# The order of GpSimd's gathers and the units of VectorE's additions in a decoder layer with an expert feed-forward

## The chip, the core and the metric

The kernel runs on one core of one Trainium2 chip. The metric is the device time of one execution in microseconds; a kernel's number is the median of its runs. Lines are those of the kernel before.

## What is computed

One decoder layer on 256 tokens of width 2048, float32 in and out. The first half (an input projection, two kinds of causal convolution, an output projection, a layer norm) gives x1. The second half is a feed-forward block with 16,384 experts, of which every token picks 16 in each of 8 heads:

```python
experts = e1 * N_KEYS + e2            # 128 picks for each token
act = gelu(einsum('td,thkd->thk', x_tok, peer_u[experts]))
coef = act * softmax(top_s)
f = einsum('thk,thkd->td', coef, peer_v[experts])
x = layer_norm(ALPHA * x1 + f, ln2_g, ln2_b)
```

## The kernel before

**Units.** All weights come in units of 128 x 1024 floats (512 KB), loaded by SyncE into a ring of four (`raw`). A product keeps float32 precision by splitting each unit: ScalarE rounds it (`w_hi`, L575), VectorE (L815) or GpSimd (L500) makes the rest (`w_lo`), and TensorE multiplies both parts. Everything is written against a unit number u. VectorE splits unit u + 3 at its turn u, so it is at most three units ahead of TensorE; both rings have four places.

**The up stage** (U_UP on) multiplies x1 with all 16,384 columns of `u_w`, tile by tile of 128 experts. For the first 192 tokens the activations are kept dense and multiplied with dense gates. For the last 64 tokens (SPARSE) ScalarE puts the activations of every expert into `stage` and from there into DRAM (`act_spill`).

**The down stage** (U_DOWN to U_END, 256 units) multiplies the dense coefficients of 192 tokens with `v_w`: 32 groups of four tiles, 8 units a group, each unit ten matmuls of 128x512 (L1576 to L1581). Coefficients of the next group are split at each group's first unit (ScalarE L728 and L729, VectorE L1234 and L1235). The last four groups are ordered by columns instead (U_LAST = U_DOWN + 224), so that results are folded and normalized early.

**The last 64 tokens** take another way in that stage. Each has 128 picks, laid out as 64 picks (PICKS) over two halves of the partitions. For pick k GpSimd issues indirect DMAs:

- `gather_acts` (L536, DMA at L538): one DMA fetches the 128 activations of pick k (4 bytes for each partition) from `act_spill`. Sixteen of them (PICKS_IN) raise one semaphore, `act_in[n]`. VectorE waits for it once per sixteen picks (`pick_coefs`, L1278) and makes sixteen columns of coefficients at once (L1279).
- `gather_rows` (L525, DMAs at L532): four DMAs fetch the row of `v_w` for each partition, 512 floats each, into one of four buffers (`rows`, ROWS = 4). Row k waits until pick k - 4 is done with the buffer. The first two rows are fetched in the up stage.

VectorE adds the row, times its coefficient, to `picked` in `pick(k)` (L1281; L1288 for k = 0, else L1291). The pick stands in VectorE's instruction stream at unit `pick_unit(k)`, behind the split of unit u + 3 and the coefficient split, if one is there:

```python
            for u in range(U_DOWN, U_END):
                if u + LEAD < U_END:
                    lo(u + LEAD, u + LEAD)
                ...
                if u in coef_at:
                    coef_lo(coef_at[u])
                for k in range(PICKS):
                    if pick_unit(k) == u:
                        pick(k)
```

GpSimd does nothing else in this stage until the final layer norm. Its order is written out by hand: rows 0 and 1, acts 0 to 15, rows 2 and 3; then acts 16 to 31 and rows 4 to 11; acts 32 to 47 and rows 12 to 19; acts 48 to 63 and rows 20 to 63. When all 64 picks are done (ScalarE waits for it in `split_high(0)`, L761, in unit U_LAST + 11), `picked` is split and folded into the result by matmuls.

Of the kernel before, what the change touches and what calls it, by code (L numbers as in the profile page):

```python
# [33 lines left out]
PICKS = HEADS * TOPK // HALVES  # L34
ROWS = 4
PICKS_IN = 16
# [24 lines left out]
U_DOWN = U_UP + 2 * N_KEYS  # L61
# [15 lines left out]
U_LAST = U_DOWN + 2 * NCH * G_LAST  # L77
# [28 lines left out]

def pick_unit(k):

    return U_DOWN + 14 + (U_LAST - U_DOWN - 16) * k // PICKS

PC_B = 0
PC_CW = PC_B + 2 * CONF_TILES + 3 * SC_TILES
# [8 lines left out]
def build(nc, x_t, x_nat, w_in, w_out, w_q, u_w, v_w, params, sub_keys, b_out, ln1_g, ln1_b, ln2_g, ln2_b, out):  # L121
# [11 lines left out]
    with ctx:  # L133
        def sb(name, shape, dt, where=ctx):
            return where.enter_context(nc.sbuf_tensor(name, shape, dt))

        def sem(name):
            return ctx.enter_context(nc.semaphore(name))
# [119 lines left out]
        sp_idx = sb("sp_idx", [P, 1 + NCH, PICKS], u32)  # L258
# [117 lines left out]
        act_in = [sem(f"act_in{i}") for i in range(PICKS // PICKS_IN)]  # L376
# [25 lines left out]
        def vector_takes(u):  # L402


            if u < U_CONV:
                return True
            if U_Q <= u < U_ROUTED:
                return False
            return u >= U_ROUTED or u % 2 == 0
# [67 lines left out]
        @block.gpsimd  # L477
        def _(pool):
            nc.gpsimd.iota(iota[:, :], [[1, P]], base=0, channel_multiplier=0,
                           allow_small_or_imprecise_dtypes=True).then_inc(iota_done, 1)  # L480
            pool.wait_ge(iota_done, 1)
            nc.gpsimd.tensor_copy(iota_t[:, :, :], iota[:, :].unsqueeze(2).to_broadcast([P, P, INNER]))\
                .then_inc(iota_done, 1)
            nc.gpsimd.memset(ident[:, :], 0.0).then_inc(pool_done, 1)
            nc.gpsimd.memset(ones[:, :], 1.0 / (CONF_TILES * P)).then_inc(pool_done, 1)
            nc.gpsimd.memset(apad[:, :, 0:TAPS - 1], 0.0).then_inc(pool_done, 1)
            nc.gpsimd.memset(scpad[:, 0:SC_TAPS - 1], 0.0).then_inc(pool_done, 1)
            pool.wait_ge(pool_done, 4)
            nc.gpsimd.affine_select(out=ident[:, :], in_=ident[:, :], compare_op=ALU.not_equal, fill=1.0,
                                    base=0, pattern=[[-1, P]], channel_multiplier=1).then_inc(pool_done, 1)  # L490

            def stream_rest(first, end):

                assert first % RAW == 0 and end % RAW == 0
                with pool.Fori(first // RAW, end // RAW) as i:
                    for s in range(RAW):
                        if not vector_takes(end - RAW + s):

                            pool.wait_ge(hi_done, RAW * i + s + 1)
                            nc.gpsimd.tensor_tensor(w_lo[s][:, :], raw[:, s, :], w_hi[s][:, :].bitcast(f32),  # L500
                                                    ALU.subtract).then_inc(lo_done[s], SPLIT)

            first_loop = -(-U_CONV // RAW) * RAW
            for u in range(U_CONV, first_loop):
                if not vector_takes(u):
                    pool.wait_ge(hi_done, u + 1)
                    nc.gpsimd.tensor_tensor(w_lo[u % SPLIT][:, :], raw[:, u % RAW, :],
                                            w_hi[u % SPLIT][:, :].bitcast(f32),
                                            ALU.subtract).then_inc(lo_done[u % SPLIT], SPLIT)
            stream_rest(first_loop, U_Q)  # L510
            stream_rest(U_Q, U_UP)


            pool.wait_ge(x1_out, 16)
            nc.gpsimd.iota(sp_tok[:, 0:1], [[1, 1]], base=0, channel_multiplier=1,
                           allow_small_or_imprecise_dtypes=True).then_inc(tok_done, 1)
            nc.gpsimd.memset(fold_f, 0.0).then_inc(fold_made, 1)
            pool.wait_ge(fold_made, 1)
            nc.gpsimd.tensor_tensor(fold_f[:, SPARSE:2 * SPARSE], ident[:, 0:SPARSE], ident[:, SPARSE:P],
                                    ALU.add).then_inc(fold_made, 1)  # L520
            pool.wait_ge(fold_made, 2)
            nc.gpsimd.tensor_copy(fold[:, :], fold_f).then_inc(fold_made, 1)
            stream_rest(U_UP, U_ROUTED)

            def gather_rows(k):  # L525

                if k >= ROWS:
                    pool.wait_ge(picked_done, k - ROWS + 1)
                elif k >= 2:
                    pool.wait_ge(used, USED0 + U_DOWN)  # L530
                for j in range(NCH):
                    nc.gpsimd.indirect_dma_start(  # L532
                        rows[k % ROWS][:, j * DCH:(j + 1) * DCH], None, v_rows,
                        bass.IndirectOffsetOnAxis(sp_idx[:, 1 + j, k:k + 1], 0)).then_inc(rows_in[k % ROWS], 16)

            def gather_acts(n):  # L536
                for k in range(PICKS_IN * n, PICKS_IN * (n + 1)):
                    nc.gpsimd.indirect_dma_start(  # L538
                        sp_act[:, k:k + 1], None, act_dram,
                        bass.IndirectOffsetOnAxis(sp_idx[:, 0, k:k + 1], 0)).then_inc(act_in[n], 16)  # L540

            pool.wait_ge(idx_done, 1)
            pool.wait_ge(sel_tr, 1)
            for k in range(2):
                gather_rows(k)
            pool.wait_ge(stage_out, 16 * (N_KEYS // STORED))
            gather_acts(0)
            for k in range(2, ROWS):
                gather_rows(k)
            for n in range(1, PICKS // PICKS_IN):  # L550
                gather_acts(n)
                for k in range(ROWS + 8 * (n - 1), ROWS + 8 * n):
                    gather_rows(k)
            for k in range(ROWS + 8 * (PICKS // PICKS_IN - 1), PICKS):
                gather_rows(k)

            pool.wait_ge(ln2_in, 32)
            for n, (b, d) in enumerate(LN2_POOL):
                sl = slice(d * DCH, (d + 1) * DCH)
                pool.wait_ge(normed, 2 * n + 2)  # L560
                nc.gpsimd.tensor_tensor(res[:, b, sl], res[:, b, sl], ln2g[:, sl], ALU.mult).then_inc(pool_ln, 1)
                pool.wait_ge(pool_ln, n + 1)
                nc.gpsimd.tensor_tensor(res[:, b, sl], res[:, b, sl], ln2b[:, sl], ALU.add).then_inc(fin_pool, 1)
# [240 lines left out]
        def _(dve):  # L804
# [529 lines left out]
# [3 lines that stand above are left out]
                if u == U_DOWN:  # L1337
                    gate_tile_of(N_KEYS - 1)
# [5 lines that stand above are left out]
                if u in split_at and u < U_END - 2 * LAST:  # L1344
                    split_low(split_at[u])
                j, n = (u - U_LAST) // (2 * LAST), (u - U_LAST) % (2 * LAST)
                if u >= U_LAST and 1 <= j < NCH - 1 and n < 2:
                    dve.wait_ge(used, USED0 + U_LAST + 2 * LAST * j)
                    if n == 0:
                        dve.wait_ge(res_in, 16)  # L1350
                        added = add_down(0, j - 1)
                    else:
                        chunk_stats(0, j - 1, chain[0], x2_in)
                if u >= U_LAST and j == 2 and n == 5:
                    add_folded(0)
# [340 lines left out]
```

## Time and profile before

| | us |
|---|---|
| median of 3 runs | 1906.56 |
| lowest and highest run | 1905.19, 1913.26 |
| profiled execution | 1898.23 |
| its span, first to last instruction | 1896.4 |
| TensorE busy | 1779.9 (94%) |
| VectorE busy | 1363.7 (72%) |
| GpSimd busy | 670.2 (35%) |

The mean granted clock of TensorE is 0.978 of its full 2.4 GHz. A busy time is the time in which an engine had an instruction running. Matmuls overlap and their ends are modelled, so the sum over lines is more than the busy time. "Issue" is time in which an engine waited for nothing that the profile shows. The down stage lies between about 1175 us and the end.

### The profile page before, as it was taken

To read this page: it belongs to the slowest core of one execution; us is meant where nothing else is said; L and a number is where in the kernel's file an instruction comes from. 1 tells how busy PE (TensorE), PEld (TensorE's weight loads), DVE (VectorE), ACT (ScalarE), POOL (GpSimd) and SP (SyncE) were. 2 spreads that over 40 slices of the span, in tenths; PEclk is the share of its full clock that TensorE was granted. 3 is DMA by queue.
4 is the path that set the end of the run, shared out by engine and by line. 5 is a ranking of instruction groups with operands and counts; after the bars stand their busy time and mean duration, and the time that the engine had idled before them with its cause. 6 is when DMAs were issued, how large, how long until landed. Compare 5 with 4: busy or idle time off the path is not lost.

```text
span 1896.4 us, 33625 instructions
## 1 busy us (share of the span) xinstructions
PE 1779.9 (94%) x12090; PEld 1627.9 (86%) x12090; DVE 1363.7 (72%) x1903; ACT 855.4 (45%) x1212; POOL 670.2 (35%) x425
## 2 busy tenths in 40 slices
PE   8999999899999999999999999969695999999996
PEld 8999978899999999999999999847574777777875
DVE  7998985699937777777764445557483787888866
ACT  5544444444444444444444444524242445444443
POOL 0000024678961000000000000677786787777201
PEclk9999999999999999999999999989897999999999
DMA  7665556555566555555556565769695999999863
GB/s 277 225 211 191 184 167 215 189 173 175 170 209 229 183 182 186 183 181 188 181 189 194 191 193 191 230 201 332 220 346 187 383 350 369 332 348 366 293 210 114
DMA packets 137934, 433.27 MB, mean 228 GB/s; under 512 B 34304, under 2 KB 34432, under 8 KB 136320
## 3 DMA queue, kind: packets, MB, share of 16 engines
q1 hardware_dynamic: 97440, 359.97, 55.9%
q0 software_dynamic: 22528, 67.16, 9.7%
q10 hardware_dynamic: 17888, 5.26, 1.2%
q8 instruction: 30, 0.49, 0.1%
q14 instruction: 48, 0.39, 0.1%
HBM read 423.83 MB, written 8.39 MB: 228 GB/s over the span
## 4 chain that ended last, share of the span: by engine, by line
PE 71%; POOL 11%; issue 8%; DMA 5%; DVE 4%; ACT 2%; SPq 0%; DVEq 0%; POOLq 0%; ACTq 0%
PE psum L1409 18%; PE psum L1410 18%; PE psum L1411 18%; POOL rows L532 5%; DMA raw<-in_v_w_dram 4%; POOL sp_act L538 4%; PE psum L1576 3%; PE psum L1578 2%; PE psum L1577 2%; PE psum L1580 2%; PE psum L1581 2%; DVE w_lo L815 2%; PE psum L1543 1%; PE psum L1453 1%; PE psum L1455 1%
## 5 line engine op out<-in xcount | busy, mean ns | idle before, releaser
L575 ACT ACTIVATE w_hi<-raw 128x1024 fp32r<-128x1024 f32 x652 | 691.2, 1061 | 936.4 <-PE psum L1411 484.3
L815 DVE TENSOR_TENSOR w_lo<-raw,w_hi 128x1024 fp32r<-128x1024 f32 x568 | 688.6, 1224 | 310.3 <-ACT w_hi L575 303.3
L1409 PE MATMUL psum<-xt_hi,w_hi 128*128 128x256 f32 x2944 | 827.1, 281 | 15.5 <-DVE xt_lo L829 9.3
L1410 PE MATMUL psum<-xt_lo,w_hi 128*128 128x256 f32 x2944 | 824.6, 280 | 0.0
L1411 PE MATMUL psum<-xt_hi,w_lo 128*128 128x256 f32 x2944 | 823.7, 280 | 0.0
L1409 PEld LDWEIGHTS psum<-xt_hi,w_hi 128*128 128x128 f32 x2944 | 555.2, 189 | 17.4 <-issue 11.5
L1411 PEld LDWEIGHTS psum<-xt_hi,w_lo 128*128 128x128 f32 x2944 | 555.1, 189 | 0.0
L1410 PEld LDWEIGHTS psum<-xt_lo,w_hi 128*128 128x128 f32 x2944 | 555.0, 189 | 0.0
L532 POOL DMA_INDIRECT rows<-in_v_w_dram,sp_idx x256 | 364.4, 1423 | 148.1 <-issue 101.6
L538 POOL DMA_INDIRECT sp_act<-act_spill,sp_idx x64 | 78.6, 1228 | 626.2 <-DMA act_spill<-stage 585.5
L1576 PE MATMUL psum<-w_hi,c_hi 128*128 128x512 f32 x504 | 204.3, 405 | 78.9 <-DVE w_lo L815 76.7
L500 POOL TENSOR_TENSOR w_lo<-raw,w_hi 128x1024 fp32r<-128x1024 f32 x82 | 211.4, 2593 | 74.1 <-ACT w_hi L575 73.6
L1291 DVE SCALAR_TENSOR_TENSOR picked<-rows,sp_coef,picked 128x2048 f32<-128x2048 f32 x63 | 148.4, 2356 | 76.0 <-DMA rows<-in_v_w_dram,sp_idx 51.0
L1577 PE MATMUL psum<-w_lo,c_hi 128*128 128x512 f32 x504 | 201.8, 400 | 0.0
L1578 PE MATMUL psum<-w_hi,c_lo 128*128 128x512 f32 x504 | 201.5, 400 | 0.0
L1580 PE MATMUL psum<-w_hi,c_both 128*128 128x512 f32 x504 | 201.2, 399 | 0.0
L1581 PE MATMUL psum<-w_lo,c_both 128*128 128x512 f32 x504 | 201.0, 399 | 0.0
L1576 PEld LDWEIGHTS psum<-w_hi,c_hi 128*128 128x128 f32 x504 | 96.1, 191 | 109.9 <-DVE w_lo L815 84.0
L1578 PEld LDWEIGHTS psum<-w_hi,c_lo 128*128 128x128 f32 x504 | 96.3, 191 | 23.4
L1580 PEld LDWEIGHTS psum<-w_hi,c_both 128*128 128x128 f32 x504 | 96.1, 191 | 23.5 <-DVE w_lo L815 0.2
L1581 PEld LDWEIGHTS psum<-w_lo,c_both 128*128 128x128 f32 x504 | 95.8, 190 | 23.2
L1577 PEld LDWEIGHTS psum<-w_lo,c_hi 128*128 128x128 f32 x504 | 96.3, 191 | 22.2
(193 smaller groups left out, 1165.1 us busy)
## 6 DMA issues: line engine op xcount, KB each, us to landing
raw<-in_u_w_dram SPq DMA_DIRECT2D x256, 512.0 KB
raw<-in_v_w_dram SPq DMA_DIRECT2D x256, 512.0 KB
raw<-in_w_in_dram SPq DMA_DIRECT2D x80, 512.0 KB
raw<-in_w_out_dram SPq DMA_DIRECT2D x32, 512.0 KB
raw<-in_w_q_dram SPq DMA_DIRECT2D x32, 512.0 KB
act_spill<-stage ACTq DMA_DIRECT2D x32, 128.0 KB, 2.3
rows<-in_v_w_dram,sp_idx POOLq DMA_INDIRECT x256
xt_raw<-in_x_t_dram SPq DMA_DIRECT2D x4, 512.0 KB, 7.5
```

The source lines that it names most:

```text
L500: nc.gpsimd.tensor_tensor(w_lo[s][:, :], raw[:, s, :], w_hi[s][:, :].bitcast(f32), ALU.subtract).then_inc(lo_done[s], SPLIT)
L532: nc.gpsimd.indirect_dma_start(rows[k % ROWS][:, j * DCH:(j + 1) * DCH], None, v_rows, bass.IndirectOffsetOnAxis(sp_idx[:, 1 + j, k:k + 1] ...
L575: nc.scalar.activation(parts_of(slot_u)[0][:, :], raw[:, slot_u % RAW, :], ACT.Copy).then_inc(hi_done, 1)
L815: tt(lo_w[:, :], raw[:, slot_u % RAW, :], hi_w[:, :].bitcast(f32), ALU.subtract).then_inc(lo_done[slot_u % SPLIT], SPLIT)
L1409: mm(dst, hi_w[:, sl], xt_hi[:, kk, :], start=st, stop=False)
L1410: mm(dst, hi_w[:, sl], xt_lo[:, kk, :], start=False, stop=False)
L1411: i = mm(dst, lo_w[:, sl], xt_hi[:, kk, :], start=False, stop=en)
L1576: mm(v_bank(j, 0), hi_c[:, n, :], w1, start=st, stop=False)
L1577: mm(v_bank(j, 0), hi_c[:, n, :], w2, start=False, stop=False)
L1578: i = mm(v_bank(j, 0), lo_c[:, n, :], w1, start=False, stop=en)
L1580: mm(v_bank(j, 1), both_c[:, n, :], w1, start=st, stop=False)
L1581: i = mm(v_bank(j, 1), both_c[:, n, :], w2, start=False, stop=en)
```

## The change

The acts of picks 16 to 63 are no longer issued as three batches of sixteen in front of rows 4, 12 and 20. After each row from row 4 on, one or two acts are issued (four for three rows), until all 64 are out after row 39. `act_in[n]` still stands for sixteen acts. And `pick_unit` places pick k at unit 20 + 212k/64 of the down stage, where it was 14 + 208k/64, rounded down: pick 0 moves from unit 14 to 20, pick 63 from 218 to 228.

```diff
 def pick_unit(k):
 
-    return U_DOWN + 14 + (U_LAST - U_DOWN - 16) * k // PICKS
+    return U_DOWN + 20 + (U_LAST - U_DOWN - 12) * k // PICKS
+
+
+def acts_issued(k):
+
+    return min(PICKS, PICKS_IN + (4 * max(0, k - ROWS + 1) + 2) // 3)
...
-            def gather_acts(n):
-                for k in range(PICKS_IN * n, PICKS_IN * (n + 1)):
+            def gather_acts(first, end):
+                for k in range(first, end):
                     nc.gpsimd.indirect_dma_start(
                         sp_act[:, k:k + 1], None, act_dram,
-                        bass.IndirectOffsetOnAxis(sp_idx[:, 0, k:k + 1], 0)).then_inc(act_in[n], 16)
+                        bass.IndirectOffsetOnAxis(sp_idx[:, 0, k:k + 1], 0)).then_inc(act_in[k // PICKS_IN], 16)
...
-            gather_acts(0)
+            gather_acts(0, PICKS_IN)
             for k in range(2, ROWS):
                 gather_rows(k)
-            for n in range(1, PICKS // PICKS_IN):
-                gather_acts(n)
-                for k in range(ROWS + 8 * (n - 1), ROWS + 8 * n):
-                    gather_rows(k)
-            for k in range(ROWS + 8 * (PICKS // PICKS_IN - 1), PICKS):
+            for k in range(ROWS, PICKS):
                 gather_rows(k)
+                gather_acts(acts_issued(k - 1), acts_issued(k))
```

## Rows read from the trace of the kernel before

**Rows 1.** The page's slices (40 equal slices of the span, busy tenths).
```profile
PE   8999999899999999999999999969695999999996
DMA  7665556555566555555556565769695999999863
```
**Rows 2.** Waits of 1250 to 1896 us: total, times, longest.
```profile
PE psum L1576 <- DVE w_lo L815: 76.7, 14, 23.1
DVE picked L1291 <- DMA rows<-in_v_w_dram,sp_idx: 51.0, 3, 26.1
```
**Rows 3.** VectorE's timeline at picks 0, 4, 12, 20: start, length, [idle before].
```profile
1225.31 0.17 DVE L1279 TENSOR_TENSOR sp_coef<-sp_act,sp_sel 128x16 f32<-128x16 f32 x1 [3.97 <-DMA sp_act<-act_spill,sp_idx]
1225.52 1.44 DVE L1288 TENSOR_SCALAR picked<-rows,sp_coef 128x2048 f32<-128x2048 f32 x1
...
1273.10 2.35 DVE L1291 SCALAR_TENSOR_TENSOR picked<-rows,sp_coef,picked 128x2048 f32<-128x2048 f32 x1 [20.81 <-issue]
...
1357.15 2.35 DVE L1291 SCALAR_TENSOR_TENSOR picked<-rows,sp_coef,picked 128x2048 f32<-128x2048 f32 x1 [19.24 <-DMA rows<-in_v_w_dram,sp_idx]
...
1447.38 2.35 DVE L1291 SCALAR_TENSOR_TENSOR picked<-rows,sp_coef,picked 128x2048 f32<-128x2048 f32 x1 [26.09 <-DMA rows<-in_v_w_dram,sp_idx]
```
**Rows 4.** GpSimd's timeline: last of row 3, first of 4, first and last of 12.
```profile
1234.68 1.97 POOL L532 DMA_INDIRECT rows<-in_v_w_dram,sp_idx  x1 [0.30 <-issue]
...
1265.48 0.95 POOL L532 DMA_INDIRECT rows<-in_v_w_dram,sp_idx  x1 [0.30 <-issue]
...
1349.54 0.95 POOL L532 DMA_INDIRECT rows<-in_v_w_dram,sp_idx  x1 [0.30 <-issue]
...
1353.28 0.96 POOL L532 DMA_INDIRECT rows<-in_v_w_dram,sp_idx  x1 [0.30 <-issue]
```
**Rows 5.** GpSimd's groups in 1237 to 1593: count | busy us, mean ns | idle before.
```profile
L532 POOL DMA_INDIRECT rows<-in_v_w_dram,sp_idx x148 | 208.9, 1411 | 59.8 <-issue 59.8
L538 POOL DMA_INDIRECT sp_act<-act_spill,sp_idx x48 | 58.4, 1217 | 29.0 <-issue 29.0
```
**Rows 6.** VectorE's timeline at picks 40, 43 and 63.
```profile
1610.62 2.34 DVE L1291 SCALAR_TENSOR_TENSOR picked<-rows,sp_coef,picked 128x2048 f32<-128x2048 f32 x1
...
1632.35 2.41 DVE L1291 SCALAR_TENSOR_TENSOR picked<-rows,sp_coef,picked 128x2048 f32<-128x2048 f32 x1
...
1788.37 2.35 DVE L1291 SCALAR_TENSOR_TENSOR picked<-rows,sp_coef,picked 128x2048 f32<-128x2048 f32 x1
```
**Rows 7.** The chain of waits, two matmuls ten apart: start, length.
```profile
1780.02 0.23 PE psum L1581
...
1782.35 0.23 PE psum L1581
```
**Rows 8.** Stretches: length, busy PE, PEld, DVE, ACT, POOL (instructions), clock, DMA share, GB/s.
```profile
1237.00:1593.00 356.00, 286.40 (x1184) 226.98 (x1183) 235.45 (x187) 137.91 (x149) 267.23 (x196) 0.91 0.82 295
1358.00:1408.00 50.00, 44.95 (x183) 35.69 (x184) 38.49 (x33) 19.39 (x21) 39.91 (x25) 0.93 0.95 353
1497.00:1585.00 88.00, 87.19 (x374) 69.66 (x373) 72.90 (x58) 42.23 (x45) 68.61 (x48) 1.00 0.98 362
...
1790.00:1850.00 60.00, 57.71 (x246) 45.58 (x245) 37.26 (x38) 28.93 (x33) 0.00 (x0) 1.00 0.69 222
1313.00:1318.00 5.00, 5.00 (x17) 3.94 (x16) 5.00 (x4) 1.69 (x2) 4.11 (x3) 0.66 0.90 311
1694.00:1699.00 5.00, 4.67 (x20) 3.82 (x21) 5.00 (x5) 2.12 (x2) 4.39 (x3) 1.00 0.70 247
```
**Rows 9.** The page's costliest groups: VectorE's split of a unit.
```profile
L815 DVE TENSOR_TENSOR w_lo<-raw,w_hi 128x1024 fp32r<-128x1024 f32 x568 | 688.6, 1224 | 310.3 <-ACT w_hi L575 303.3
```
**Rows 10.** TensorE's timeline behind two short waits.
```profile
1312.62 0.50 PE L1576 MATMUL psum<-w_hi,c_hi 128*128 128x512 f32 x1 [2.29 <-DVE w_lo L815]
...
1694.33 0.50 PE L1576 MATMUL psum<-w_hi,c_hi 128*128 128x512 f32 x1 [1.94 <-DVE w_lo L815]
```
**Rows 11.** The chain of waits from 1600 to 1700 us, by line.
```profile
by line: DMA raw<-in_v_w_dram 49.7%; issue 24.4%; DVE w_lo L815 12.9%; ACT w_hi L575 6.5%; PE psum L1576 1.4%; SPq L418 1.3%; ACT c_hi L728 1.2%; PE psum L1578 1.2%; PE psum L1577 1.2%; PE psum L1580 1.2%; DVE picked L1291 1.1%; PE psum L15
```

## The prediction

> **What bounds the kernel now.** I read the page's slices first: TensorE is busy in nearly every slice, with one dip between the 26th and the 32nd, and in that dip the DMA engines are not full, while behind it they are [rows 1]. So the kernel runs at TensorE's pace except in the first half of the stage that adds the expert values. Next the waits of that stage: matmuls wait 76.7 us for VectorE's low parts, and VectorE waits 51.0 us in three waits for gathered rows of v_w [rows 2]. VectorE works in order, so a `pick` whose row has not landed holds up the splits behind it. Its timeline shows where: 20.8 us before pick 4 (the view calls that one "issue"), 19.2 before pick 12, 26.1 before pick 20, and 4.0 at the first coefficients [rows 3]. Picks 4, 12 and 20 are the ones whose rows stand behind sixteen `gather_acts`. GpSimd's timeline shows the other side: row 4 is issued only from 1265.5, row 12 from 1349.5, each after its batch, and each pick starts as its row lands [rows 4].
>
> What sets that pace is the number of instructions. In the 356 us from 1237 to 1593 GpSimd issues 148 row and 48 activation DMAs, 1.82 us each, with nothing before them but "issue" [rows 5]: it is simply busy. The 196th is the last of row 40. Its pick starts at 1610.6 [rows 6], so by then GpSimd is ahead, and VectorE no longer waits.
>
> **The change, step by step.** No operation is added or removed: 64 activation DMAs, 256 row DMAs, 64 picks, all as before. Two things move. (a) The acts are spread, four to three rows, so that row k stands behind 4(k - 3) row DMAs, its own included, and about 1.33(k - 4) acts, counted from row 3. All 64 are out with row 39, and with row 40 both kernels have issued the same 40 x 4 - 12 = 148 and 48. (b) Pick k moves from unit 14 + 3.25k to 20 + 3.3125k: pick 0 six units later, pick 40 eight (144 to 152), pick 63 ten (218 to 228, four into the last stage).
>
> *Start.* Row 3 is out at 1236.65 [rows 4]. Row 4 is next now, and waits for pick 0. Before, pick 0's turn had come 4.0 us ahead of its coefficients, at 1221.3 [rows 3]. A unit is ten matmuls of TensorE, 1782.35 - 1780.02 = 2.33 us [rows 7]. Six units later is 1235.3, and with 1.44 for the pick 1236.8. So the later start costs GpSimd nothing, and it covers the 4.0 us.
>
> *The old stalls.* With the gathers in flow a unit takes (1788.4 - 1632.4)/65 = 2.40 us (picks 43 and 63, units 153 and 218 [rows 6]). Row 4 is out after 4 DMAs, about 1245, and its pick is due at 1235.3 + 13 x 2.40 = 1267: the 20.8 us are gone. Row 12 stands behind 47 DMAs, 1237 + 47 x 1.83 + 3 = 1326, against a turn at 1331: gone too. Then GpSimd falls behind: with acts a row costs it 5.33 x 1.83 = 9.76 us, and picks are 3.3125 x 2.40 = 7.95 apart. From about pick 15 to pick 40 each waits some 1.8 us. That is what is late next: three long waits become a trickle.
>
> *The pace* is the price that decides. With VectorE idle an issue takes 0.95 + 0.30 = 1.25 us [rows 4]. In the dearest stretch, 1358 to 1408, 25 issues take 50 us, 2.01 each; in 1497 to 1585, 48 take 88 us, 1.83 each, VectorE being busy 73 of 88 [rows 8]. The change takes away VectorE's long quiet, in which issues are cheap, yet leaves it no busier than 3.31 x 1.224 [rows 9] + 2.35 for the pick + some 0.4 for coefficients = 6.8 us in 9.76, 70%. I take 1.83, the busy stretch, next to 1.82 over all. Ends: 1.66 (busy time and bare steps of 0.30 alone, (208.9 + 58.4)/196 + 0.30 [rows 5]) and 2.01.
> [...]
>
> *The gain at pick 40.* Row 40 is out at 1237 + 196 x 1.83 = 1595.7, and a pick that waits starts 2.9 us after its row is out (row 12: out at 1354.24, pick at 1357.15 [rows 3, 4]). So pick 40, and with it unit 152, comes at 1598.6. Before, unit 152 was one unit ahead of pick 43: 1632.4 - 2.4 = 1630.0 [rows 6]. **Gain 31 us.** 19 of it (8 units) come from the later schedule and 15 from the lead that stood idle at pick 40 (1610.6 - 1593 - 2.9), less 3 for the pace. Spreading the acts is what lets both be used, as pick 20 would otherwise stand behind 116 DMAs and set the stall.
>
> *What is given back.* At unit 152 the old kernel had some 18 rows left to issue, the new one 23. A row is 1.05 MB (four DMAs of 128 x 512 floats); at the 362 GB/s of 1497 to 1585 (DMA share 0.98 [rows 8]) five rows are 14.5 us of transfer. In 1600 to 1700 half of the chain is raw weight loads [rows 11], so they would be felt there; from 1790 the share is 0.69 and there is room [rows 8]. Bounds 0 and 14.5; I take 7, the middle. The last two picks now lie at units 225 and 228, beside coefficient splits for which TensorE waits: 2 x 2.35 us on a VectorE busy 37 of 60 us [rows 8], so 0 to 4.7; I take 1.5. ScalarE's wait for all 64 picks is seven units behind the last, which hides it; were that gone, pick 63 would be paid again at 2.35. SP's queue is not moved.
>
> **Sum:** 31 - 7 - 1.5 = 22.5 us. The profiled execution took 1898.2 us, which becomes 1875.7; the median of the runs is 1906.6, 8.3 above it, so the forecast there is **1884 us**.
>
> **Rivals.**
> 1. *Transfers eat the gain.* For it: DMA share 0.98 once the gathers flow, raw loads on the chain [rows 8, 11]. Against: 0.82 over 1237 to 1593. All 14.5 us and all 4.7 are paid: gain 12, 1894.6.
> 2. *Interleaved acts issue more cheaply.* The 48 acts carry 29.0 us of gaps [rows 5] where bare steps make 14.4. If the rest belongs to batches, 14.6 us more come, less 3 for transfers: 1872.5.
> 3. *Slower: the clock.* Where TensorE had waited 2.29 us, the clock was at 1.2 GHz for (1 - 0.66) x 2 x 5 = 3.4 us of the next 5; where it had waited 1.94, it stayed at 2.4 GHz [rows 8, 10]. The trickle makes 25 such waits. A pick's units need 3.3125 x 2.33 = 7.7 us of TensorE in 9.76, so 2.0 us are spare: 4 us at half clock decide. One fall of 3.4 us per pick is hidden; two cost 1.4 us x 25 = 34: 1918. Against: the wait at 1694 did nothing.
> [...]
> 4. *The pace is 2.01* without VectorE's quiet: pick 40 at 1633.9, 4 us later than before, and 8.5 given back: 1919.
> 5. *Nothing moves,* since the count at row 40 is the same and something else binds at the same place: 1906.
>
> **Chances.** Forecast 0.58, rival 1 0.16, rival 2 0.12, rival 3 0.06, rival 4 0.05, rival 5 0.03. The range goes past rival 2 (a pace of 1.75 and 4 given back make 42) and up to a gain of 3.6: 1864 to 1903. A measurement of this kernel tells about 0.5%, 9.5 us. Faster by more: nearly all of the forecast and rival 2, most of rival 1, 0.80; within, 0.11; slower, 0.09.
>
> **What would show it.** No wait of VectorE over 10 us for a gathered row, none at pick 4; small waits from about pick 15 to 40, some 47 us in all (pick 40 at 1598.6 against 1235.3 + 132 x 2.40 = 1552) where it was 77 of delay (1610.6 against 1221.3 + 130 x 2.40); row 40 out near 1596; matmul waits for the low part many and short; clock near 1.0; DMA share of 1237 to 1593 near 0.87. Wrong would be waits of the old length, row 40 out after 1610 (the pace), a clock below 0.9 beside waits under 3 us, or units over 2.45 us behind pick 40.

## The result, and the profile after

The changed kernel takes 2011.4 us (median of 4 runs, 2005.8 to 2014.1), the kernel before 1909.3 beside it: a ratio of 1.053 with a 95% interval of 1.050 to 1.057. It is slower by 5%, where 1884 us was forecast. The profiled execution has a span of 2007.8 us. All executions are fast ones, but for one of the four of the kernel with 768 under "The size of the queue", which took 7706 us in a slow state of the core, is unexplained and is left out. Lines of the kernel have moved: the row DMAs are L537 (L532 before), the activation DMAs L543 (L538), the pick L1293 (L1291), the split L817 (L815).

The slices of the changed kernel, against [rows 1]:

```profile
PE   8999998999999999999999999966766676799996
PEclk9999999999999999999999999988887888899999
DMA  7665546555666555555556568875675665799973
```

There is no longer a dip but a plateau: from slice 27 to 35 TensorE is busy six or seven tenths, and the DMA engines stand at five to seven where they had been full. The waits from 1250 us on, against [rows 2] (total, times, longest):

```profile
DVE picked L1293 <- issue: 227.8, 33, 10.3
...
PE psum L1578 <- DVE w_lo L817: 136.5, 33, 8.3
...
DVE picked L1293 <- DMA rows<-in_v_w_dram,sp_idx: 1.0, 3, 0.5
```

The forecast's shape is there: no wait of 20 us, many short ones. Its size is not. VectorE waits 228.8 us for rows in 36 waits, some 6 us each, where 47 us in waits of 1.8 were expected. GpSimd's groups from row 4 to row 40, against [rows 5], and two stretches, against [rows 8]:

```profile
L537 POOL DMA_INDIRECT rows<-in_v_w_dram,sp_idx x149 | 253.4, 1700 | 182.4 <-issue 179.2 <-DVE picked L1290 3.2
L543 POOL DMA_INDIRECT sp_act<-act_spill,sp_idx x48 | 48.8, 1017 | 14.6 <-issue 14.6
```
```profile
1238.00:1734.00 496.00, 365.30 (x1325) 282.83 (x1324) 258.79 (x208) 153.83 (x167) 301.57 (x197) 0.86 0.67 227
1734.00:1903.00 169.00, 163.21 (x680) 130.16 (x680) 134.81 (x106) 77.39 (x83) 131.98 (x88) 0.97 0.94 345
```

The same instructions that took 356 us now take 496, 2.52 us each. Of that, 302.2 us are busy and 197 x 0.30 = 59 are the bare steps (the 0.30 us that lie between any two of GpSimd's DMAs): together 361 us, 1.84 for each of the 197. Of the other 138 us of idle time 3 are a wait for pick 0; for the rest no other engine answers. The DMA engines are not the reason, at a share of 0.67; behind row 40, with the acts gone, 88 issues take 169 us, 1.92 each, and the stops are few and at most 2.4 us long, much as in the kernel before at the same place (89 in 169 us).

Where that idle time lies is plain in GpSimd's timeline of three rows (start, length, [idle before]), and VectorE's in the same stretch:

```profile
1351.52 0.94 POOL L543 DMA_INDIRECT sp_act<-act_spill,sp_idx  x1 [0.30 <-issue]
1352.77 0.94 POOL L537 DMA_INDIRECT rows<-in_v_w_dram,sp_idx  x1 [0.30 <-issue]
1357.35 2.70 POOL L537 DMA_INDIRECT rows<-in_v_w_dram,sp_idx  x1 [3.65 <-issue]
1360.36 1.97 POOL L537 DMA_INDIRECT rows<-in_v_w_dram,sp_idx  x1 [0.30 <-issue]
1362.63 1.97 POOL L537 DMA_INDIRECT rows<-in_v_w_dram,sp_idx  x1 [0.30 <-issue]
1364.90 0.94 POOL L543 DMA_INDIRECT sp_act<-act_spill,sp_idx  x1 [0.30 <-issue]
1366.15 0.95 POOL L543 DMA_INDIRECT sp_act<-act_spill,sp_idx  x1 [0.30 <-issue]
1371.07 2.70 POOL L537 DMA_INDIRECT rows<-in_v_w_dram,sp_idx  x1 [3.97 <-issue]
...
1384.46 2.69 POOL L537 DMA_INDIRECT rows<-in_v_w_dram,sp_idx  x1 [4.99 <-issue]
```
```profile
1356.88 2.35 DVE L1293 SCALAR_TENSOR_TENSOR picked<-rows,sp_coef,picked 128x2048 f32<-128x2048 f32 x1 [7.86 <-issue]
1359.15 4.63 DVE L817 TENSOR_TENSOR w_lo<-raw,w_hi 128x1024 fp32r<-128x1024 f32 x4
1370.60 2.35 DVE L1293 SCALAR_TENSOR_TENSOR picked<-rows,sp_coef,picked 128x2048 f32<-128x2048 f32 x1 [6.82 <-issue]
...
1383.98 2.35 DVE L1293 SCALAR_TENSOR_TENSOR picked<-rows,sp_coef,picked 128x2048 f32<-128x2048 f32 x1 [6.69 <-issue]
```

Once a row GpSimd stops, here for 3.6 to 5 us (2.2 to 7.8 over all of rows 8 to 40), in front of a row's first or second DMA, and goes on 0.47 us after VectorE has begun the pick of the last row that is out in full. Of the 33 stops in rows 8 to 40, 32 end 0.45 to 0.49 us after a pick has begun. By that, both wait for the same thing: the landing of that row. (Here 1352.77 is row 13's first DMA, 1357.35 its second; pick 12 begins at 1356.88.) So GpSimd issues, waits until the row that it issued has landed, and issues again; up to row 40 it does not get ahead.

The kernel before has such stops too, which the prediction had taken as the batches' own. In its first batch of acts:

```profile
1190.31 0.94 POOL L538 DMA_INDIRECT sp_act<-act_spill,sp_idx  x1 [585.49 <-DMA act_spill<-stage]
...
1204.60 1.23 POOL L538 DMA_INDIRECT sp_act<-act_spill,sp_idx  x1 [3.43 <-issue]
...
1219.47 0.94 POOL L538 DMA_INDIRECT sp_act<-act_spill,sp_idx  x1 [4.31 <-issue]
```

They come after seven acts and after fourteen, in each batch, and where rows alone are issued they come at the fourth DMA of a row, short (0.5 to 2.8 us) or not at all.

### The profile page after: what moved, and what is told of

It reads as the page before. It is cut to its first block, busy times and chain, and to the rows that moved or that the text cites. A ratio compares the mean times of both kernels' runs of the same rounds, so it can differ in the third digit from the quotient of the medians.

```text
span 2007.8 us, 33625 instructions
## 1 busy us (share of the span) xinstructions
PE 1828.7 (91%) x12090; PEld 1660.2 (83%) x12090; DVE 1365.9 (68%) x1903; ACT 855.2 (43%) x1212; POOL 707.6 (35%) x425
## 4 chain that ended last, share of the span: by engine, by line
PE 65%; POOL 18%; issue 12%; DVE 2%; DMA 1%; ACT 1%; POOLq 0%; DVEq 0%; SPq 0%; ACTq 0%
PE psum L1411 17%; PE psum L1413 17%; PE psum L1412 17%; POOL rows L537 15%; PE psum L1578 2%; PE psum L1580 2%; PE psum L1579 2%; POOL sp_act L543 2%; PE psum L1582 2%; PE psum L1583 2%; PE psum L1545 1%; PE psum L1455 1%; PE psum L1457 1%; PE psum L1456 1%; DMA raw<-in_v_w_dram 1%
## 5 line engine op out<-in xcount | busy, mean ns | idle before, releaser
L817 DVE TENSOR_TENSOR w_lo<-raw,w_hi 128x1024 fp32r<-128x1024 f32 x568 | 687.8, 1226 | 286.9 <-ACT w_hi L577 278.9
L537 POOL DMA_INDIRECT rows<-in_v_w_dram,sp_idx x256 | 411.4, 1607 | 267.2 <-issue 223.9
L1578 PE MATMUL psum<-w_hi,c_hi 128*128 128x512 f32 x504 | 219.4, 435 | 140.1 <-DVE w_lo L817 136.5
L1293 DVE SCALAR_TENSOR_TENSOR picked<-rows,sp_coef,picked 128x2048 f32<-128x2048 f32 x63 | 148.1, 2351 | 228.8 <-issue 227.8
L543 POOL DMA_INDIRECT sp_act<-act_spill,sp_idx x64 | 69.2, 1082 | 609.9 <-DMA act_spill<-stage 584.8
L1578 PEld LDWEIGHTS psum<-w_hi,c_hi 128*128 128x128 f32 x504 | 103.0, 204 | 179.9 <-DVE w_lo L817 151.7
L1579 PE MATMUL psum<-w_lo,c_hi 128*128 128x512 f32 x504 | 213.3, 423 | 0.0
L1580 PE MATMUL psum<-w_hi,c_lo 128*128 128x512 f32 x504 | 211.3, 419 | 0.0
L1582 PE MATMUL psum<-w_hi,c_both 128*128 128x512 f32 x504 | 209.7, 416 | 0.0
L1583 PE MATMUL psum<-w_lo,c_both 128*128 128x512 f32 x504 | 209.0, 415 | 0.0
L1580 PEld LDWEIGHTS psum<-w_hi,c_lo 128*128 128x128 f32 x504 | 103.5, 205 | 26.0
L1579 PEld LDWEIGHTS psum<-w_lo,c_hi 128*128 128x128 f32 x504 | 103.9, 206 | 23.1
```

The lines of the kernel that those rows point to most:

```text
L537: nc.gpsimd.indirect_dma_start(rows[k % ROWS][:, j * DCH:(j + 1) * DCH], None, v_rows, bass.IndirectOffsetOnAxis(sp_idx[:, 1 + j, k:k + 1] ...
L817: tt(lo_w[:, :], raw[:, slot_u % RAW, :], hi_w[:, :].bitcast(f32), ALU.subtract).then_inc(lo_done[slot_u % SPLIT], SPLIT)
L1578: mm(v_bank(j, 0), hi_c[:, n, :], w1, start=st, stop=False)
L1579: mm(v_bank(j, 0), hi_c[:, n, :], w2, start=False, stop=False)
L1580: i = mm(v_bank(j, 0), lo_c[:, n, :], w1, start=False, stop=en)
L1582: mm(v_bank(j, 1), both_c[:, n, :], w1, start=st, stop=False)
```

## The experiments

Three theories could explain this; all are guesses until the runs below.

**Theory A.** GpSimd's queue has few places, about seven DMAs. When it is full, GpSimd waits for a landing; and it can take back places only up to a DMA whose semaphore no later DMA in the queue raises. The four DMAs of a row share a semaphore, so only the fourth counts; the acts of a batch share one, so none counts while another is in the queue. With rows alone, GpSimd stands at DMA 4 of row k with seven in the queue and waits for DMA 4 of row k - 1: three have been issued behind it, which covers most of a landing. With acts between, the seven in front of row 13's second DMA are act 26, row 12's four, act 27 and row 13's first: it waits for row 12's fourth, with two behind it.

**Theory B.** The row lands late because VectorE, held up, splits three or four units at once behind each pick, and the weight loads that this sets free go in front of the row.

**Theory C.** The later units do the harm.

### One half of the change each

The changed kernel with the old units:

```diff
-    return U_DOWN + 20 + (U_LAST - U_DOWN - 12) * k // PICKS
+    return U_DOWN + 14 + (U_LAST - U_DOWN - 16) * k // PICKS
```

> The changed order of acts and rows with the old units (pick k at unit 14 + 3.25k). Theory A (GpSimd's queue holds only few DMAs, about seven, and gives places back only when the last DMA of a semaphore in it has landed; with acts between the rows, GpSimd stops once a row until the row just issued has landed): the step of 13.7 us from pick to pick between picks 12 and 40 stays, row 40 is out as late as in the changed kernel, and its unit is 8 units earlier, so about 2025 us. Theory B (the row lands late because VectorE splits three or four units at once behind each pick, and their weight loads go in front of it): the same, 2010 to 2030. Theory C (the later units do the harm): near 1907.

Measured: 2039.7 us (2033.0 to 2040.6), 1.068 [1.064, 1.073] of before. That is above what theories A and B gave; the step from pick to pick stayed at 13.6 us, as both said. And the kernel before with the new units (the same edit the other way round):

> The old order with the new units. Theories A and B: the order did all the harm; pick 20, behind the third batch, is still the one that waits, but seven units later, so 12 to 17 us are gained: 1890 to 1895. Theory C: near 2000.

Measured: 1894.1 us (1887.1 to 1896.7), 0.993 [0.990, 0.995]. So theory C falls: the later units are worth 14 us on the old order and 28 on the new, and the order alone costs 132. In this last kernel, with the old order and the new units, VectorE's waits at picks 12 and 20 are 44 us together, where they were 45 before [rows 3]:

```profile
1367.77 2.35 DVE L1291 SCALAR_TENSOR_TENSOR picked<-rows,sp_coef,picked 128x2048 f32<-128x2048 f32 x1 [25.01 <-issue]
...
1450.62 2.35 DVE L1291 SCALAR_TENSOR_TENSOR picked<-rows,sp_coef,picked 128x2048 f32<-128x2048 f32 x1 [19.22 <-DMA rows<-in_v_w_dram,sp_idx]
```

### The same DMAs in the same order, with other semaphores

Each of a row's four DMAs raises a semaphore of its own, and the sixteen acts of a batch take four semaphores in turn. VectorE waits for all of them.

```diff
-        act_in = [sem(f"act_in{i}") for i in range(PICKS // PICKS_IN)]
+        act_in = [[sem(f"act_in{n}_{i}") for i in range(4)] for n in range(PICKS // PICKS_IN)]
...
-        rows_in = [sem(f"rows_in{i}") for i in range(ROWS)]
+        rows_in = [[sem(f"rows_in{i}_{j}") for j in range(NCH)] for i in range(ROWS)]
...
-                        ...).then_inc(rows_in[k % ROWS], 16)
+                        ...).then_inc(rows_in[k % ROWS][j], 16)
...
-                        ...).then_inc(act_in[k // PICKS_IN], 16)
+                        ...).then_inc(act_in[k // PICKS_IN][k % 4], 16)
...
-                dve.wait_ge(act_in[n], 16 * PICKS_IN)
+                for i in range(4):
+                    dve.wait_ge(act_in[n][i], 16 * PICKS_IN // 4)
...
-                dve.wait_ge(rows_in[k % ROWS], 16 * NCH * (k // ROWS + 1))
+                for j in range(NCH):
+                    dve.wait_ge(rows_in[k % ROWS][j], 16 * (k // ROWS + 1))
```

> The changed kernel, the same DMAs in the same order, but each of a row's four DMAs raises a semaphore of its own (16 for the four buffers), and the acts of a batch go round four semaphores. Theory A: any of the DMAs in the queue can now be the one whose place is given back, GpSimd waits only for the oldest of seven, the gaps of 3 to 5 us once a row go, and a row costs it 9 to 10 us: 1880 to 1895, as was forecast blind. Theory B: nothing changes, 2011.

Measured: 1853.6 us (1850.3 to 1856.5), 0.971 [0.967, 0.975]. 158 us less than the changed kernel, though no instruction of work, no byte and no order has changed; better than expected. Theory B expected 2011 and falls. GpSimd's groups, from row 4 to row 40:

```profile
L537 POOL DMA_INDIRECT rows<-in_v_w_dram,sp_idx x148 | 214.3, 1448 | 53.8 <-issue 44.8 <-DVE picked L1292 9.0
L543 POOL DMA_INDIRECT sp_act<-act_spill,sp_idx x48 | 71.8, 1496 | 14.6 <-issue 14.6
```

The idle time is 196 x 0.30 = 59 us and the 9.0 of the wait for pick 0; the stops are gone. The stretch from row 4 to row 40, and pick 40:

```profile
1235.00:1581.00 346.00, 319.68 (x1306) 253.25 (x1306) 256.42 (x203) 150.89 (x162) 286.12 (x196) 0.95 0.90 318
```
```profile
1586.67 2.35 DVE L1295 SCALAR_TENSOR_TENSOR picked<-rows,sp_coef,picked 128x2048 f32<-128x2048 f32 x1
```

196 issues take 346 us, 1.76 each, and pick 40 comes at 1586.7, where the changed kernel has it at 1739.1:

```profile
1739.10 2.35 DVE L1293 SCALAR_TENSOR_TENSOR picked<-rows,sp_coef,picked 128x2048 f32<-128x2048 f32 x1 [6.21 <-issue]
```

The two halves of the edit, each alone. First the lines of `act_in`:

> The changed kernel with four semaphores in turn for the acts of a batch; the rows' four DMAs share one as before. Theory A in its narrow form (a place is given back only at a DMA whose semaphore no later one in the queue raises): an act between two rows can now be given back alone, so GpSimd reaches one DMA further before it must wait for the last DMA of the row before: three issued behind it instead of two. A landing takes 5 to 6 us and three issues 4 to 6, so most of the gap goes but not all: 1865 to 1920. Wide form (only the number of DMAs in flight counts, not who shares a semaphore): 2011.

Measured: 1918.0 us (1912.7 to 1922.8), 1.007 [1.005, 1.009]. GpSimd's timeline, from row 12's third DMA to row 13's:

```profile
1321.87 1.05 POOL L537 DMA_INDIRECT rows<-in_v_w_dram,sp_idx  x1 [2.58 <-issue]
1323.22 0.96 POOL L537 DMA_INDIRECT rows<-in_v_w_dram,sp_idx  x1 [0.30 <-issue]
1324.49 1.19 POOL L543 DMA_INDIRECT sp_act<-act_spill,sp_idx  x1 [0.30 <-issue]
1325.98 1.96 POOL L537 DMA_INDIRECT rows<-in_v_w_dram,sp_idx  x1 [0.30 <-issue]
1328.24 1.97 POOL L537 DMA_INDIRECT rows<-in_v_w_dram,sp_idx  x1 [0.30 <-issue]
1331.48 2.72 POOL L537 DMA_INDIRECT rows<-in_v_w_dram,sp_idx  x1 [1.27 <-issue]
```

The stop has moved by one DMA, from the second of row 13 to the third, where theory A puts it if act 26 can now be taken back by itself, and it has shrunk from 3.65 us to 1.27. Such a stop remains in nearly every row (0.5 to 3.4 us), and in rows 4 to 40 the idle time beyond bare steps and the wait for pick 0 falls from 135 us to 49. Then the lines of `rows_in`:

> The changed kernel with a semaphore for each of a row's four DMAs; the acts share theirs as before. Narrow form of theory A: GpSimd waits for one of the older row DMAs, with six issued behind it or close to it, and the acts are given back with the row DMA behind them: nearly all of the gain of the kernel with both, 1850 to 1870. Wide form: 2011.

Measured: 1854.1 us (1846.4 to 1863.6), 0.974 [0.969, 0.979]: all of the gain. The first batch of acts, whose semaphore is still shared, still has its stop after seven acts, where the run before this one has none:

```profile
1203.65 1.11 POOL L543 DMA_INDIRECT sp_act<-act_spill,sp_idx  x1 [3.54 <-issue]
```

If only the number of DMAs in flight counted, and not who shares a semaphore, both halves would have taken 2011 us; they did not.

### The size of the queue

The changed kernel with another `dynamic_dma_scratch_size`. That this sets the size of theory A's queue is a guess until the run; in proportion to the seven DMAs of the traces it would be 7 x 1536/1024 = 10.5, so ten:

```diff
-    nc = _bacc.Bacc("TRN2", target_bir_lowering=False, num_devices=1, dynamic_dma_scratch_size=1024)
+    nc = _bacc.Bacc("TRN2", target_bir_lowering=False, num_devices=1, dynamic_dma_scratch_size=1536)
```

> [...] Theory A: ten DMAs fit where seven did, so GpSimd, when it stops, has issued five behind the row it waits for instead of two, and most of the landing time is covered: 1885 to 1910, gaps short. Theory B: 2011.

Measured: 1859.5 us (1854.5 to 1861.7), 0.974 [0.970, 0.978], below the range expected. Between rows 4 and 40 four stops are left, of 2.1 us at most. The first stop now comes after ten acts, where it came after seven:

```profile
1203.95 0.94 POOL L543 DMA_INDIRECT sp_act<-act_spill,sp_idx  x1 [0.30 <-issue]
1207.97 0.94 POOL L543 DMA_INDIRECT sp_act<-act_spill,sp_idx  x1 [3.08 <-issue]
```

And the kernel before, by the same edit with 768 (7 x 768/1024 = 5.25, so five):

> [...] Theory A: five DMAs fit where seven did, so GpSimd must wait for the last DMA of each row with one issued behind it, all through the 60 rows: a step of 12 to 14 us per row as in the changed kernel, 2050 to 2150. Theory B or anything that sits in VectorE's burst or the weight loads: 1907.

Measured: 2207.5 us (2204.2 to 2207.8, three executions), 1.159 [1.154, 1.164]. The direction is as expected, the size is not: I had not put the batches' own stalls on top of the slower rows. In its first batch of acts the stops come after five, ten and fifteen (4.08, 3.83 and 2.68 us), where they came after seven and fourteen. In the timelines of GpSimd and VectorE, at rows 28 and 29:

```profile
1639.19 1.16 POOL L532 DMA_INDIRECT rows<-in_v_w_dram,sp_idx  x1 [0.30 <-issue]
1645.32 2.72 POOL L532 DMA_INDIRECT rows<-in_v_w_dram,sp_idx  x1 [4.97 <-issue]
```
```profile
1644.86 2.35 DVE L1291 SCALAR_TENSOR_TENSOR picked<-rows,sp_coef,picked 128x2048 f32<-128x2048 f32 x1 [5.32 <-issue]
...
1657.89 2.35 DVE L1291 SCALAR_TENSOR_TENSOR picked<-rows,sp_coef,picked 128x2048 f32<-128x2048 f32 x1 [7.27 <-issue]
```

With 768, the kernel without any act between its rows stops at the second DMA of row 29 until row 28 has landed, with one issued behind it, again 0.46 us after the pick has begun. It runs in the step of the changed kernel (1657.89 - 1644.86 = 13.0 us from pick to pick).

### The halves of the change, without GpSimd's stops

All three have the semaphores of the edit above, for acts and rows. The old order with the new units:

> The old order (three batches of sixteen acts) with the new units and semaphores of their own for acts and rows. It asks what the order itself is worth once GpSimd does not stop. Pick 20 stands behind 116 issues at about 1.77 us: row out near 1441 against a turn near 1405, so VectorE still loses 35 to 40 us there, where the interleaved order loses about as much in small waits up to pick 40. Theory A: 1860 to 1880, at most 1.5% behind the interleaved order. If the order were worth what the blind forecast gave it, 15 to 20 us behind: 1870 to 1875. If semaphores only matter with interleaved acts: 1894, as the units alone.

Measured: 1858.9 us (1858.1 to 1860.4), 0.976 [0.973, 0.980], 1 us below the range expected. The kernel before, nothing else changed:

> The kernel before, order and units untouched, with semaphores of their own for acts (four in turn) and rows. Theory A: the full stops in the batches go (after seven acts GpSimd waited until all seven had landed) and with them the short stops at a row's fourth DMA; pick 20 waits for 116 issues at about 1.77 instead of 1.82 us and the act batches at about 1.6, so 10 to 25 us are gained: 1880 to 1897; the units then give the rest down to 1859. If only the new units make room for it: 1907.

Measured: 1873.4 us (1872.3 to 1874.8), 0.984 [0.980, 0.987], 7 us below the range expected. The changed order with the old units:

> The changed order and semaphores of its own, with the old units. It prices the later units with GpSimd unstopped. GpSimd still runs at 1.76 us a step, picks up to 40 are eight units (19 us) earlier in the stream and wait longer for the same rows: 1864 to 1875. If VectorE's room is what counts: 1853, the same as with the new units.

Measured: 1862.1 us (1859.5 to 1864.6), 0.978 [0.974, 0.981], 2 us below the range expected. Medians in us:

| | shared semaphores | semaphores of their own |
|---|---|---|
| old order, old units (before) | 1905 to 1909 | 1873.4 |
| old order, new units | 1894.1 | 1858.9 |
| new order, old units | 2039.7 | 1862.1 |
| new order, new units (the change) | 2011.4 | 1853.6 |

So the order is worth 11 us at the old units and 5 at the new, the units 15 and 9. Of these four only the 15 is clear of the intervals of the ratios; for the other three the intervals overlap, though the executions of the two kernels do not. That is what the two ideas bring when GpSimd does not stop: 20 us together. And both remedies together:

> The changed kernel with semaphores of its own for every DMA and 1536 bytes as well. Theory A: with own semaphores the queue of seven showed bare steps of 0.30 us everywhere, so more room can bring nothing: 1850 to 1857, the same as own semaphores alone. If the queue still binds: below 1848.

Measured: 1851.3 us (1845.1 to 1858.9), 0.973 [0.969, 0.978], within the intervals of either remedy alone: with the semaphores there is no stop left between rows 4 and 40 that more places could take away. This, all semaphores alone and the rows' semaphores alone are the fastest versions, 50 to 54 us under the kernel before.

## Why the prediction was wrong

**The step that failed** is "I take 1.83, the busy stretch, next to 1.82 over all", with the ends 1.66 and 2.01: the pace of GpSimd was read as a price of one instruction, which the instruction would keep wherever it stood. It was 2.52, past both ends. The price itself was right: without the stops the changed kernel's issues cost 1.84. What was missed is that part of the idle time in [rows 5] (30 of 88.8 us, beyond 196 x 0.30) was waiting, and that the change alters what it waits for. The trace of the kernel before had the sign: a stop after exactly seven acts, twice in every batch. Rival 2 looked at those very gaps and drew the opposite from them, that they belong to batches and would go if the batches did. By theory A they belong to a full queue. In a batch it is waited for twice in 16 issues; interleaved, once in 5.33.

**Point by point.**
- *The start* was right to 2 us: pick 0 began at 1237.0, not 1235.3, row 4 waited 3.2 us for it, and pick 4 waited for nothing.
- *Waits from about pick 15* began with pick 9 (0.5 us at pick 8), and pick 40 came at 1739.1 instead of 1598.6, 140 us late. This is more than the whole miss of 134 us in the span (2007.8 against 1873.9).
- *The landing*, 2.9 us from a row's last DMA to its pick, was taken from a stall in which the weight loads stood still: between 1354.2 and 1357.2 the gathers' queue is the only one that moved data, at 220 GB/s. With them flowing it is 5.7 (row 12 was out at 1351.2, and up to 1356.9 the weight loads' queue moved 0.69 MB beside the gathers' 0.94). This too went into the stops.
- *What is given back* was too dear. From unit 152 to the end of the span the kernel before takes 1896.4 - 1630.0 = 266.4 us, the changed one 2007.8 - 1739.1 = 268.7, so 2.3 us where I took 8.5; with semaphores of their own it is 1853.9 - 1586.7 = 267.2, 0.8 us. The five rows more cost almost nothing.
- *Rival 1* (transfers) and *rival 4* (a pace of 2.01) did not come: without the stops an issue cost 1.84, those beside a busy VectorE among them. *Rival 3* ended on the right side for the wrong reason. The clock fell, to a mean of 0.86 over 1238 to 1734, but 13.7 us a pick leave TensorE 6 us to spare, and the clock stood at 0.95 in the same stretch once the stops were gone: it followed the waits. The fall that the rival reads from the mean of 0.66 is one to half the clock: between 1314 and 1317 us of the kernel before the granted clock is 0.50, and matmuls of 512 columns start 0.427 us apart, where it is 0.233 at a clock of 1.00. Its 1.2 GHz, and the 2.4 of the full clock, are an estimate from that step (512 / 0.427 = 1.2 columns in a ns, taken as one in a cycle, and twice that).
- *The forecast's mechanism* holds with the stops taken out, and so does its size. Row 40 is out at 1581, where 1595.7 was forecast, and VectorE waits 45.9 us for rows in 14 waits, where 47 were forecast. The 1853.6 us are not all its doing: the kernel before had stops of its own, worth 32 us, and without them the change brings 1873.4 - 1853.6 = 20 us, where 22.5 were forecast.
- *"Spreading the acts is what lets both be used"* is not borne out. Without the stops the new units on the old order reach 1858.9 us, within 5 us of the whole change.

**How sure the cause is.** Shown: the stops end just behind the start of a pick, so with a landing (32 of 33); they depend on `dynamic_dma_scratch_size` (five, seven and ten DMAs before the first stop with 768, 1024 and 1536) and on which DMAs share a semaphore, at an unchanged order; the place of the stop moves by one DMA where theory A says so. Not shown is the queue itself: the profile has no record of it, and calls all of this "issue". Whether a place is always one DMA is open, as every DMA here fetches 128 pieces, one for each partition.

## What to carry to other kernels

In these kernels idle time of GpSimd in front of an indirect DMA, put down to "issue" and longer than the bare step of 0.30 us, went with its own earlier DMAs: in 32 of 33 stops it ended 0.45 to 0.49 us behind the start of the pick whose row had landed. Where you see the same, count the DMAs between such stops, and look whether each stop ends together with a landing. Then try semaphores of their own for DMAs that are in flight together (here 2011.4 us became 1853.6), or let the ones sharing a semaphore stand together. An innocent DMA put between two groups can cost more than the stall that it was moved to avoid: here the acts between the rows cost 132 us, against stalls of 20.8, 19.2 and 26.1 us [rows 3]. A price per instruction read from one order of a queue holds for another only when its idle part is explained: here 1.82 us became 2.52.

## What had not been expected of the hardware

- Semaphores alone moved this kernel by 158 us (2011.4 to 1853.6), and a `dynamic_dma_scratch_size` of 1536 instead of 1024 by 152 (to 1859.5). With 768, 1024 and 1536 GpSimd issued five, seven and ten DMAs before its first stop.
- How long an issue of GpSimd takes goes with what VectorE does beside it. In the changed kernel the row DMA issued at 1357.35, 0.47 us into a pick, takes 2.70 us and ends 0.8 us after the pick (1359.2). The next two issues, beside the four splits from 1359.15 on, take 1.97 us each; the two behind the splits, with VectorE idle, 0.94 and 0.95. From 1180 to 1740 us the 89 issues that VectorE's instructions overlap by less than 0.05 us take 0.94 to 0.96, the 45 beside a pick 2.50 in the mean and up to 4.22, and the 90 beside other instructions of VectorE 1.56 and up to 1.99. The profile does not say what holds them up.
